# Router logits from the raw residual, the first gather from the rank product, the gather at the head of a turn

## The reference, cut to what matters

```python
for layer in range(2):
    h = rmsnorm(x, norm_mix[layer])
    out = ab_mixer(h, ...) if layer == 0 else gdn_mixer(h, ...)
    x = x + out
    h = rmsnorm(x, norm_ffn[layer])
    x = x + hier_moe(h, ...)
y = rmsnorm(x, norm_final)

def rmsnorm(x, g):
    return x * rsqrt(mean(x * x, axis=-1) + 1e-6) * g

def hier_moe(x, ...):                     # x (288, 1024)
    p_grp = softmax(x @ w_grp + b_grp)    # 4 groups: the best one
    fine = (x @ w_exp + b_exp) of that group          # 8 experts: the best two
    gate = p_sel * w_top / sum(w_top)
    # rows sorted by expert, padded to blocks; per block
    hb = silu(xb @ w_gate[e]) * (xb @ w_up[e])
    out_rows = hb @ w_down[e]             # 1024 -> 512 -> 1024
    # back to the tokens, weighted by gate
```

## Time and profile before

| | us |
|---|---|
| median of 3 runs (1702.12 to 1702.74) | 1702.45 |
| profiled execution, own time | 1703.48 |
| its span, first to last instruction | 1701.4 |
| TensorE busy | 1279.6 (75%) |
| VectorE busy | 579.7 (34%) |
| ScalarE busy | 256.3 (15%) |
| mean rate of all transfers | 268 GB/s |

### The profile page before, as it was taken

How to read it: one execution, slowest core, us unless ns; L and a number is a source line. 1 busy time by engine, 2 the same in 40 slices (tenths; PEclk the granted TensorE clock), 3 DMA queues, 4 the chain that set the end, 5 groups by cost and what they waited for, 6 DMA issues and landing times.

```text
span 1701.4 us, 26209 instructions
## 1 busy us (share of the span) xinstructions
PE 1279.6 (75%) x10786; PEld 844.9 (50%) x10786; DVE 579.7 (34%) x1369; ACT 256.3 (15%) x627; POOL 81.6 (5%) x110
## 2 busy tenths in 40 slices
PE   5998976666677677767997978987676676776675
PEld 3776743544344344434774866764443444344343
DVE  2023455421322122123445665555512220222122
ACT  2122112110111011101213122132010110111011
POOL 2000102000000000002001010012000000000000
PEclk9999898798888788887998999987787997888887
DMA  9641115399999999997331000024299999999993
GB/s 287 170 100 57 56 56 232 140 426 427 428 425 426 426 426 427 425 426 249 103 133 67 1 1 1 1 112 164 106 425 426 426 426 427 427 426 427 426 426 158
DMA packets 61523, 455.93 MB, mean 268 GB/s; under 512 B 5456, under 2 KB 6000, under 8 KB 28576
## 3 DMA queue, kind: packets, MB, share of 16 engines
q1 hardware_dynamic: 59216, 449.35, 65.4%
q0 software_dynamic: 2256, 5.88, 1.3%
HBM read 451.87 MB, written 3.35 MB: 268 GB/s over the span
## 4 chain that ended last, share of the span: by engine, by line
PE 52%; DMA 31%; DVE 10%; issue 3%; ACT 2%; POOL 1%; SPq 1%; DVEq 0%; ACTq 0%; POOLq 0%
PE bank L259 50%; DMA W<-in_moe_w_up 30%; PE bank L262 2%; DVE HN L994 1%; DVE X L1495 1%; POOL sm L1622 1%; DVE zT L954 1%; DVE W L954 1%; DMA X<-in_x_prompt 1%; SPq L1566 1%; DVE HN L954 1%; DVE HN L974 0%; DVE TM L954 0%; DVE zT L1423 0%; DVE zT L1456 0%
## 5 line engine op out<-in xcount | busy, mean ns | idle before, releaser
L259 PE MATMUL bank<-W,zT 128*32 128x256 f32 (+1 forms) x6400 | 527.1, 463 | 199.8 <-DMA W<-in_moe_w_up 167.5
L259 PEld LDWEIGHTS bank<-W,zT 128*32 128x32 f32 (+1 forms) x6400 | 266.7, 132 | 430.0 <-issue 312.2
L259 PE MATMUL bank<-HT,W 128*128 128x294 f32 x896 | 229.2, 415 | 2.4 <-ACT zT L765 1.5
L259 PEld LDWEIGHTS bank<-HT,W 128*128 128x128 f32 x896 | 170.2, 191 | 56.8 <-issue 3.8
L1438 DVE TENSOR_TENSOR zT<-zT,bank 64x256 f32<-64x256 f32 x64 | 27.1, 423 | 399.7 <-ACT zT L929 399.0
L259 PE MATMUL bank<-zT,HN 128*128 128x128 f32 x864 | 105.4, 284 | 12.1 <-DVE zT L1427 12.1
L259 PEld LDWEIGHTS bank<-zT,HN 128*128 128x128 f32 x864 | 102.0, 199 | 19.1 <-issue 19.1
L1449 DVE COPY zT<-bank 32x256 f32<-32x256 f32 x128 | 53.3, 417 | 160.7 <-PE bank L259 158.7
L259 PE MATMUL bank<-const,zT 64*128 64x64 f32 (+1 forms) x272 | 47.8, 297 | 78.2 <-DVE zT L1438 64.1
L259 PE MATMUL bank<-W 128*128 128x128 f32 (+2 forms) x840 | 96.5, 273 | 12.5 <-DVE W L954 8.2
L259 PEld LDWEIGHTS bank<-W 128*128 128x128 f32 (+2 forms) x840 | 89.9, 183 | 21.2 <-DVE W L954 9.4
(11 more groups left out here) (196 smaller groups left out, 1020.9 us busy)
## 6 DMA issues: line engine op xcount, KB each, us to landing
W<-in_moe_w_down SPq DMA_DIRECT2D x64, 2048.0 KB, 21.5
W<-in_moe_w_gate SPq DMA_DIRECT2D x64, 2048.0 KB, 18.6
W<-in_moe_w_up SPq DMA_DIRECT2D x64, 2048.0 KB, 23.1
W<-in_ab_w_in SPq DMA_DIRECT2D x8, 2048.0 KB, 15.9
W<-in_c_w_in SPq DMA_DIRECT2D x8, 2048.0 KB, 13.8
W<-in_ab_w_out SPq DMA_DIRECT2D x2, 2048.0 KB, 8.0
W<-in_c_w_out SPq DMA_DIRECT2D x2, 2048.0 KB, 7.6
const<-in_const SPq DMA_DIRECT2D x1, 1451.5 KB, 14.9
```

Source lines behind the costliest of these rows:

```text
L259: return nc.tensor.matmul(out, lhsT, rhs, start=start, stop=stop)
```

## The change

1. The router works on the raw residual. `flip_x` transposes X itself, tile 0 before `output_sample`; `router_logits(t)` has the tokens as the stationary side, so that the logits come out by token. The gain is multiplied into the router's weights by POOL when they arrive; `rstd` and the bias come in when VectorE takes the logits.
2. HN is needed for the gather only; ScalarE writes it (`rows_for_experts`), without the gain, which is multiplied in when the gathered rows are copied to xg.
3. The first gather's one-hot is made from the rank product alone (the first four experts' ranks), the gather starts before the block list is known, and the list's products stand between its parts. The weights of the tokens and the slots of later turns are formed after it.
4. In the loop the gather stands at the head of the turn; turn 0 is written out before the loop, and `share_rows` comes after its first expert.
5. Norms: each tile is squared as soon as it is there, VectorE and ScalarE scale one half each, the gain is multiplied in when VectorE takes the transpose. The scatter finishes tile 0, then tile 1, then tile 2.
6. A small tensor of gains by column (`gcol`) replaces the three loads of a gain of 512 KB; the final gain is loaded by POOL at the start. The input weights are read as `(k p)` instead of `(p k)`. Experts 2 and 3 are loaded without waiting for the list.

```diff
+            def flip_half(src, t, g, lane):          # TensorE: four transposes into one bank
...
             def norm():
                 for t in range(TILES):
-                    hn_ready.wait(pe)
-                    transpose_tile(lambda c: HN[:, t, c * P:c * P + P], t, N_TOK[t])
+                    hn_dve.wait(pe)
+                    flip_half(HN, t, 0, L0)
+                    hn_act.wait(pe)
+                    flip_half(HN, t, 1, L0)
                 ht_dve.wait(pe, 3)
-                ht_act.wait(pe, 3)
+            def flip_x(t):
+                x_ready.wait(pe)
+                for g in range(2):
+                    flip_half(X, t, g, L0 if t == 2 else lanes[g])
+            def router_logits(t):
+                n, c = N_TOK[t], COL[t]
+                ht_dve.wait(pe)
+                if t < 2:
+                    ht_act.wait(pe)
+                bank = L0.open(pe)
+                for k in range(KT):
+                    last = mm(bank[:n, 0:36], HT[:, k, c:c + n], small_w[:, k, 0:36], k == 0, k == KT - 1)
+                L0.close(last)
...
+                flip_x(0)                            # TensorE, end of each mixer
                 output_sample()
...
             def experts(l):                          # TensorE
-                norm()
-                small_projection(36, 1 + 2 * l, 4)
+                E["router_w"].wait(pe)
+                flip_x(1)
+                router_logits(0)
+                flip_x(2)
+                router_logits(1)
+                router_logits(2)
                 E["choice_ready"].wait(pe)
...
+                bank = side.open(pe)
+                r3 = bank[:, 0:96].rearrange("p (t e) -> p t e", e=NEXP)
+                mm(r3, tri_strict, M, True, False)
+                mm(r3[:, 1:3, :], ones, M[:, 0:1, :].to_broadcast([P, 2, NEXP]), False, False)
+                side.close(mm(r3[:, 2, :], ones, M[:, 1, :], False, True))
...
+                hn_moe.wait(pe, 3)
+                pe.wait_ge(m["onehot"], 1)
+                gather_part(range(4)).then_inc(m["gathered_lo"], 1)
+                E["nb_ready"].wait(pe)
...
+                gather_part(range(4, 6))
+                E["list_ready"].wait(pe)
...
+                gather_part(range(6, 8)).then_inc(m["gathered_hi"], 1)
+                E["blocks_ready"].wait(pe)
+                nb = nblk_reg(pe)
...
-                    for u in range(QUAD):
-                        gate_up(u, b)
-                        if u == QUAD - 1:
-                            gather(b + 2)
-                        flip_hidden(u, b)
-                        down(u, b)
+                expert(0, 0)
+                share_rows()
+                for u in range(1, QUAD):
+                    expert(u, 0)
+                scatter(0)
+                with pe.Fori(1, nb) as b:
+                    gather(b)
+                    for u in range(QUAD):
+                        expert(u, b)
                     scatter(b)
...
+            def norm(x_there):                       # ScalarE
+                x_there(0)
+                squares(0)
+                x_there(1)
+                squares(1)
+                scaled(0)
+                x_there(2)
+                squares(2)
+                scaled(1)
+                scaled(2)
...
+                x_ready.wait(act)                    # ScalarE, experts
+                squares(0)
+                take_x(0)
+                x_ready.wait(act)
+                squares(1)
                 act.wait_ge(states_out, l + 1)
+                rows_for_experts(0)
+                take_x(1)
+                x_ready.wait(act)
+                squares(2)
+                rows_for_experts(1)
+                rows_for_experts(2)
...
+                def fetched(b):                      # ScalarE, at the head of a turn
+                    act.wait_ge(m["gathered_hi"], b + 1)
+                    for k in range(4, 8):
+                        nc.scalar.activation(xg[:, k, :], banks[1][:, (k - 4) * P:(k - 3) * P], ACT.Copy,
+                                             scale=gcol[:, 4 + l, k:k + 1]
+                                             ).then_inc(m["xg_act"] if k == 7 else m["xg_act_part"], 1)
...
+            def norm(i):                             # VectorE
+                scaled(0)
+                scaled(1)
+                normalised(0, i)
+                scaled(2)
+                normalised(1, i)
+                normalised(2, i)
...
+                take_x(1)                            # VectorE, experts
+                take_logits(0)
+                take_x(2)
+                take_logits(1)
+                take_logits(2)
...
+                tt(oh4, bc_last(rank[:, :, 0:QUAD], BLK), iota32, ALU.is_equal)
+                v.tensor_tensor(oh4, oh4, bc_last(t3(M, NEXP)[:, :, 0:QUAD], BLK), ALU.mult).then_inc(m["onehot"], 1)
...
+                fetched(0)                           # VectorE, after the list; then slots, weights, diagonals
...
+                with dve.Fori(1, nb) as b:
+                    fetched(b)
+                    expert(0, b)
+                    onehot(b)
+                    shares(b)
+                    for u in range(1, QUAD):
+                        expert(u, b)
+                    adds(b)
...
-                        t, h = i % 2, i // 2         # scatter and its adds
+                        t, h = i // 2, i % 2
...
-                    dma(gain[:], row(a["norm_mix"][0]), gain0_in)
+                    dma(gcol[:], a["norm_cols"], gcol_in)
...
                 for u in (2, 3):                     # SP
-                    load(0, u)
+                    load(0, u, u)
+                E["blocks_ready"].wait(sp)
...
+            load(gain[:], a["norm_final"].partition_broadcast(P), gain_in)      # POOL, start
...
+                small_in[1 + 2 * l].wait(pool, 64)   # POOL, router_weights
+                do(nc.gpsimd.tensor_tensor(small_w[:], small_w[:],
+                                           gcol[:, 1 + 2 * l, :].unsqueeze(2).to_broadcast([P, KT, 36]), ALU.mult),
+                   E["router_w"])
```

More of the change, by code:

```diff
@@ L1372, in experts @@
[L1372 to L1382 removed]
+                tt(eq, rest, bc_last(max2, 8), ALU.is_equal)
@@ L1510, in _ @@
             experts(1)
-            norm(last=True)
+            final_norm()
         @block.sync
```

428 lines of the change are left out of this document (218 added, 210 removed).

## The result

| | before | after |
|---|---|---|
| median of the runs shown with it (us) | 1702.6 (1702.12 to 1703.2, 4 runs) | 1649.66 (1648.74 to 1652.16, 4 runs) |
| profiled execution: own time, span (us) | 1703.48, 1701.4 | 1648.74, 1646.9 |
| granted clock, mean | 0.873 | 0.882 |

The ratio is 0.9694 (0.968 to 0.9708): 3.1% faster. 1646 was predicted, within 1632 to 1667.

What follows compares the result with a forecast made beforehand. The prediction took weight transfers to fill the expert loop, leaving gains outside it. Terms of 58.2 us took the profiled 1703.48 to 1645.3, median 1644.3; 2 us for hand-offs gave 1646, range 1632 to 1667.

Steps and rivals of the forecast that it cites:

- Start: Kernel start to first projection: tile 1 arrives sooner once the gain leaves SP's queue; 6.5 us saved (3.1 to 8.2).
- The warning that the gain on GpSimd's queue might hold tile 1 to 11.9: At the start: transfers from POOL share the same 16 engines, so tile 1 may gain nothing; sum 3 us higher.
- Routing: Sample's output projection to first dependent load: earlier logits, shorter choice, gather before list; 17.3 us saved in layer 0, 16.8 in layer 1.
- The rival of the late list: In routing, the list, not the gather, ends it: 8.4 us saved shrink to 1 per layer; 1661 us, chance 0.12.
- Slow passes: Rival: TensorE stays at granted clock 0.50 through routing, with the start at its lower bound; 1661 us, chance 0.17.
- Loop: Expert loop: moving the gather to the turn's head uses first-expert weights about 2 us later, within the cover; 0 saved.
- The spare time: At the seam of two turns: the transfer line stays filled long enough to spare about 10.8 us of delay.
- the rival of the dry line: The gather at the turn's head idles the transfers, paid at 14 seams; 1719 us at 16 us delay, chance 0.04.
- After the last landing: Last turn of each layer: flip and down matmuls no longer wait behind a useless gather; 4.5 us saved per layer.
- Norm into layer C: Scatter to layer C's projection: squares, scaling and eviction run behind a scatter ending tile by tile; 5.8 us saved.
- final norm: Last scatter to the end: squares no longer wait for the last add; 2.8 us saved (1 to 4).
- two compute-bound mixers, whose inside the change hardly touches: Mixer insides: taken as hardly changed by the edit, with no saving or loss counted there.

Runs made afterwards that it cites:

- list_first: The kernel after, with the block list and TensorE's read of the block count ahead of the first gather again in both layers: 1657.95 us.
- head_thrice: The kernel after, with the gather at the head of every turn but the first done three times: 1720.3 us, ratio 1.0082 to before.
- gather_ahead: The kernel after, with the next turn's gather ahead of the last expert's flip again: 1656.03 us.
- whole_norm: The kernel after, with every tile's squares waiting for all five adds of the last scatter, ahead of layer C and at the end: 1653.99 us.
- all_three: The kernel after, with the final gain loaded later, block count read only in the first turn, ScalarE's exponentials ahead of the logarithm: 1639.01 us.

## Why the prediction was right, and where it was not

- *Start, 6.5 said, 5.7 measured.* Tile 1 came at 9.2 (9 said); what is left behind it took 7.6 instead of 7.0. The warning that the gain on GpSimd's queue might hold tile 1 to 11.9 did not come true: with that gain issued at 4.07, behind tile 1's 2.13, or without it, the squares began at 9.24 and 9.19; only ahead on the same queue did it cost 2.6. Other profiles of the same start give 4.8 to 6.0 won. The rule of the Trainium skill ("DMA: Bandwidth & Descriptors", section "Issuing engines are not separate DMA queues") says that transfers of all engines interleave on the same 16; at this place no run shows the later transfer slowing the earlier one.
- *Routing, 17.3 and 16.8 said, 17.7 and 16.9 measured.* Ahead of the choice 8.9 said, 8.5 measured; from choice to load 8.4 said, 9.2 measured. The issue came 13.7 us after the gather's start (14.5 said). The list inside the gather, with the late read, is only 2 to 3 us of that per layer (list_first); 2.1 of the 9.2 in layer 0 are the share rows, which left the path. The rival of the late list was near: the list was last, by 1.4 and 1.2 us, under the 2 us that were to decide.
- *Slow passes.* The clock was at 0.50 from 276 to 292, as that rival had it, but not in tile 0's logits (1.95 us for 16 passes) nor in the first expert (3.66). In the gather 0.20 us for each of the first 24 passes and 0.13 for the rest average to 0.17, near the 0.16 that the sum used: the term already held the slow clock. That the new routing leaves TensorE fewer pauses did not keep the clock up: TensorE waits 5.08 us for the choice.
- *Loop, 0 said, 0 measured.* The next gate weights go out 23.5 to 26.2 us after the landing instead of 22.4 to 23.9, up to 3.8 us later at the same seam (2 said). (One turn, the first of layer 1, took 59.4 us, over the 59.2 that were to decide; it took 59.7 before.) The spare time was mis-sized: 8.2 us at the seam of the earlier trace rows, not 10.8, and 5.5 are left after the change at its latest seam. What failed is the 4.9 us for a 2 MB piece alone: issued into an empty line it took 7.4 to 7.7. The price behind the edge, one us per us and seam, is as stated; head_thrice is the rival of the dry line made real, at 1720 us.
- *After the last landing, 4.5 each said, 4.9 and 5.1 measured.* gather_ahead gives 8.8 of it back, and 1.4 more by its clock. That the two figures come so near is in part luck: with the clock that the same code had in other profiles the two layers together won 5.0 to 10.2.
- *Norm into layer C, 5.8 said, 5.05 measured; final norm 2.8 said, 3.0 measured.* whole_norm takes 2.0 and 3.0 of them, but all of the 2.0 except 0.1 is made up before the next wait ends, by a projection at the full clock. Other profiles of the same code give 3.9 to 5.8 into layer C.
- *The term that was wrong: "two compute-bound mixers, whose inside the change hardly touches", with 2 us for hand-offs.* The new steps needed no such margin, the other terms sum to 58.4 against 58.2. But layer C lost 4.0 us inside. Before, the first of three table loads was done while ScalarE waited, and TensorE waited 1.48 us; after, all three stand behind the wait. From the kernel before:
```profile
799.42 1.28 ACT L747 ACT_TABLE_LOAD   x1
...
816.06 12.17 PE L259 MATMUL bank<-HT,W 128*128 128x294 f32 x48 [1.48 <-ACT zT L765]
```
  1.36 us are the longer wait and 1.67 the lower clock behind it (13.84 for the same 48 products, granted clock 0.58 in 784 to 788); all_three won both back. The last 1.0 is what is left of a first projection 0.6 shorter (5.97 instead of 6.54) and 1.6 more behind the 48 products, and was not traced. So of the 5.05 won ahead of layer C only 1.0 was left at layer 1's sample projection. Why the first load moved behind the wait no run shows; the code of the gates is the same in both kernels.

- *The number.* Of the 3.7 us between 1646 and 1649.66 the spans hold 1.7 (56.2 said, 54.5 measured). The rest is the profiled run's place among the runs: 1.0 above the median before, 0.9 below it after.

## What to carry over

Where transfers fill a loop, the time outside the loop is the kernel's to win: order it by what is ready first (raw input before its norm, a tile before the set), and sum each stretch against its own rows. Inside the loop measure the spare time at the seam, since it is free up to an edge and costs every turn behind it, and count the last moment of an issue with the time that a transfer into an empty line takes, not with the spacing of a full one. Follow a term past its own end to the next wait: us won ahead of a wait for another engine can be lost there. When the operations of an engine change, look at what that engine has to load for its next function: a table load that was hidden in a wait can come out behind it, and a short stop of TensorE can be paid again in its clock (here 1.67 us behind a stop of 2.84).

## What the runs showed of the hardware

- ScalarE's copy of 128x1024 with a scale and a transposed view takes 2.13 us, its square of the same size in order 1.06 (layer 0's routing, at 269.80 and 268.62); it was hidden here.
- In the loop the copies with a per-partition scale brought a table load with them: two per turn after (402.18 and 413.37), one before (487.04), 1.28 us each, hidden there. Behind squares the same kind of copy stood without one (759.44).
- A GpSimd power of 32 values took 1.47 us at 1641.65, while VectorE multiplied two tensors; those of 128 values at 1638.28 and 1639.99, begun ahead of such a product, took 0.55.
- TensorE's clock: the same 64 gate and up matmuls took 3.66 us at a granted clock of 1.00 (at 298.43), 4.88 at 0.74 (743.90, behind a wait of 5.32) and 6.29 at 0.58 (gather_ahead, 740.37, behind 5.61).
- A 2 MB transfer landed 4.9 us behind the one before it in a full line, but 7.4 to 7.7 us after its issue into an empty one (head_thrice).
